# A PEER gather kernel: the dots' second operand in PSUM instead of SBUF, and four PSUM banks for the rest instead of six

## The reference: what is computed

```python
def block(xb):                                   # 128 tokens
    qh = (xb @ wq).reshape(PEER_BLOCK, PEER_HEADS, 2, PEER_HALF)
    s1 = jnp.einsum('thd,nd->thn', qh[:, :, 0], keys1)
    s2 = jnp.einsum('thd,nd->thn', qh[:, :, 1], keys2)
    v1, i1 = lax.top_k(s1, PEER_TOPK)
    v2, i2 = lax.top_k(s2, PEER_TOPK)
    ...                                          # top 16 of the 16 x 16 sums: sc, e
    gate = jax.nn.softmax(sc, axis=-1)
    act = jax.nn.gelu(jnp.einsum('td,thkd->thk', xb, u_tab[e])) * gate
    return jnp.einsum('thk,thkd->td', act, v_tab[e])
```

## Time and profile before

| what | value |
|---|---|
| median of three runs | 3465.75 us (3464.83 to 3470.75) |
| span of the profiled execution | 3605.3 us |
| one block of the loop in it | 404 to 413 us |
| busy share PE, DVE, POOL, ACT | 84%, 65%, 64%, 18% |
| moved by DMA | 1213.76 MB, 337 GB/s over the span |

### The profile page before, as it was taken

The page is one execution under the profiler, slowest core; times in us unless marked ns, Lnnn a source line. Parts: engine busy times, 40 slices in busy tenths (PEclk is TensorE's granted clock), DMA queues, the critical chain, the costliest instruction groups (busy, mean ns, idle before and its releaser), DMA issues.

```text
span 3605.3 us, 39214 instructions
## 1 busy us (share of the span) xinstructions
PE 3011.3 (84%) x10724; PEld 1568.6 (44%) x10724; DVE 2354.0 (65%) x5813; ACT 658.5 (18%) x2015; POOL 2298.7 (64%) x2132
## 2 busy tenths in 40 slices
PE   7687888889987898879987798879987799877677
PEld 2553454345533454345533454345533454344222
DVE  3565975578656875578756876568655876568442
ACT  2211221112211221112211221112211121111111
POOL 0224666766777566766676567667676567667775
PEclk9799999989999999999999999999998999999999
DMA  6456989999999999999999999999999999999998
GB/s 241 161 174 240 366 316 346 371 354 351 337 372 378 348 338 351 348 361 359 330 368 357 363 314 355 361 340 369 341 353 355 364 327 345 350 375 373 355 368 296
DMA packets 340167, 1213.76 MB, mean 337 GB/s; under 512 B 41072, under 2 KB 41200, under 8 KB 339904
## 3 DMA queue, kind: packets, MB, share of 16 engines
q0 software_dynamic: 304128, 1107.43, 83.1%
q1 hardware_dynamic: 35776, 103.32, 7.7%
HBM read 1205.73 MB, written 4.87 MB: 336 GB/s over the span
## 4 chain that ended last, share of the span: by engine, by line
PE 37%; issue 20%; DMA 16%; DVE 9%; POOL 9%; another core or an unknown queue 6%; ACT 3%; POOLq 0%; ACTq 0%; SPq 0%; DVEq 0%
PE acc L428 23%; PE bank L428 13%; DMA ring<-peer_v,idx 11%; POOL ring L404 9%; DMA ring<-peer_u,idx 6%; DVE ring L1266 2%; ACT xn L750 1%; ACT diag L750 1%; DVE kw L1050 1%; DVE xn L1161 0%; DVE xn L1164 0%; ACT h L750 0%; ACT xT L750 0%; DVE topi L1052 0%
## 5 line engine op out<-in xcount | busy, mean ns | idle before, releaser
L428 PE MATMUL acc<-ring,diag 128*128 128x512 f32 (+1 forms) x4224 | 2086.7, 623 | 449.9 <-DMA ring<-peer_v,idx 269.1
L1266 DVE SCALAR_TENSOR_TENSOR ring<-ring,xcur 128x1024 f32<-128x1024 f32 x1056 | 1289.0, 1225 | 818.0 <-DMA ring<-peer_u,idx 744.5
L404 POOL DMA_INDIRECT ring<-peer_v,idx x1056 | 1151.2, 1090 | 643.6 <-issue 291.9
L404 POOL DMA_INDIRECT ring<-peer_u,idx x1056 | 1143.7, 1083 | 642.7 <-issue 316.5
L428 PEld LDWEIGHTS acc<-ring,diag 128*128 128x128 f32 (+1 forms) x4224 | 746.4, 192 | 1427.7 <-issue 1107.3
L750 ACT ACTIVATE diag<-ident,coef 128x128 f32<-128x128 f32 x1024 | 366.7, 395 | 646.7 <-PE acc L428 392.6
L428 PEld LDWEIGHTS bank<-xT,win 128*128 128x128 f32 (+1 forms) x2304 | 272.9, 183 | 79.2 <-issue 73.5
L428 PE MATMUL bank<-xT,win 128*128 128x128 f32 (+1 forms) x2304 | 282.6, 277 | 2.4 <-ACT xT L750 2.4
L750 ACT ACTIVATE G<-bank 128x128 f32<-128x128 f32 (+1 forms) x137 | 40.6, 296 | 830.4 <-PE bank L428 449.4
L428 PE MATMUL bank<-win,xT 128*128 128x512 f32 (+3 forms) x368 | 166.2, 583 | 1.9 <-ACT xT L750 1.9
L428 PEld LDWEIGHTS bank<-xT,qk 128*128 128x128 f32 x1024 | 131.5, 201 | 37.1 <-issue 37.1
(11 more groups left out here) (227 smaller groups left out, 1821.1 us busy)
## 6 DMA issues: line engine op xcount, KB each, us to landing
qk<-wq SPq DMA_DIRECT2D x64, 512.0 KB
t<-wq SPq DMA_DIRECT2D x64, 512.0 KB
ring<-peer_u,idx POOLq DMA_INDIRECT x1056
ring<-peer_v,idx POOLq DMA_INDIRECT x1056
win<-w_in SPq DMA_DIRECT2D x6, 2048.0 KB, 15.1
ring<-wq SPq DMA_DIRECT2D x16, 512.0 KB, 5.1
wout<-w_out SPq DMA_DIRECT2D x1, 4096.0 KB, 22.8
xn<-x_prompt SPq DMA_DIRECT2D x8, 512.0 KB
```

Source lines behind the costliest of these rows:

```text
L404: pool.indirect_dma_start(out=ring[:, slot, :], out_offset=None, in_=(peer_u, peer_v)[which], in_offset=bass.IndirectOffsetOnAxis(ap=idx[: ...
L428: return nc.tensor.matmul(out, lhsT, rhs, start=start, stop=stop)
L1266: stt(row, row, 1.0, xcur[:, :], ALU.mult, ALU.mult, accum_out=dots[:, column(b, e):column(b, e) + 1]).then_inc(s_dot, 1)
```

## The change

`xcur` moves from SBUF to PSUM, where it takes two banks, so that `acc` and `xcur` hold four and `bank` shrinks from six to four. The dot reads one operand from SBUF and one from PSUM; its line is otherwise unchanged. The mixer's tiles are laid anew on four banks (`xl`, the r gate and the polynomial in `bA`, gates, i gate and `v` in `bB`, `gl`, `k`, its transposes and the scores of the mLSTM in `bC`, `q`, the columns and `o` in `bD`), with a wait wherever a bank's last reader now is another one. ACT's exponential of `o` moves from tick `T_CHUNK + 8` to `T_CHUNK + 6`. The query projections use banks 2 and 3, and both halves of a head's scores lie in one bank, so that DVE waits for both in step 0.

```diff
-        xcur = sb("xcur", [P, D_MODEL])
...
+        xcur = ctx.enter_context(nc.psum_tensor("xcur", [P, D_MODEL], fp32))
-        bank = [ctx.enter_context(nc.psum_tensor(f"bank{b}", [P, 512], fp32)) for b in range(6)]
-        bA, bB, bC, bD, bE, bF = bank
+        bank = [ctx.enter_context(nc.psum_tensor(f"bank{b}", [P, 512], fp32)) for b in range(4)]
+        bA, bB, bC, bD = bank
...
                 if tick - T_K in PARTS:
...
+                        if full:
+                            pe.wait_ge(s_gl, w + 1)
-                    last = project_part(v, n, bF, 1536, f, "k")
+                    last = project_part(v, n, bC, 1536, f, "k")
...
                 if full and tick - T_V in WIDE_PARTS:
...
+                        pe.wait_ge(s_ri_exp, v + 1)
...
                 if tick == T_V + 1:
-                        pe.wait_ge(s_gl, w + 1)
+                        pe.wait_ge(s_q, w + 1)
...
                 if full and tick - T_O in WIDE_PARTS:
-                        pe.wait_ge(s_q, w + 1)
+                        pe.wait_ge(s_cols, v + 1)
...
                 if full and tick == T_CHUNK:
-                    pe.wait_ge(s_ri_exp, v + 1)
+                    pe.wait_ge(s_m2, v + 1)
...
                 if full and tick == T_CHUNK + 3:
-                    pe.wait_ge(s_lru, v + 1)
+                    pe.wait_ge(s_kw, v + 1)
...
                 if tick == T_CHUNK + 8:
...
+                    if full:
+                        pe.wait_ge(s_o, w + 1)
...
                 if tick == T_OUT - 2:
                     pe.wait_ge(s_ym, w + 1)
+                    pe.wait_ge(s_c, v + 1)
...
                 if tick == T_NORM2 + 3:
-                    pe.wait_ge(s_c, v + 1)
...
-                        last = mm(bank[4 + half][:, 0:P], wq_buf[half][:, c, :], xT[:, c, :], start=c == 0, stop=c == CM - 1)
+                        last = mm(bank[2 + half][:, 0:P], wq_buf[half][:, c, :], xT[:, c, :], start=c == 0, stop=c == CM - 1)
...
-                    mm(bank[2 * (head % 2) + half][:, 0:P], q2[:, half, :], keysT[:, half, :]).then_inc(s_score, 1)
+                    mm(bank[head % 2][:, P * half:P * half + P], q2[:, half, :], keysT[:, half, :]).then_inc(s_score, 1)
...
-                if full and tick == T_CHUNK + 8:
+                if full and tick == T_CHUNK + 6:
                     act.wait_ge(s_o_ps, w + 1)
-                    act.wait_ge(s_num_ps, w + 1)
-                    a(sigo[0:n, :, :], by4(bE)[0:n, :, :], ACT.Exp, scale=-1.0).then_inc(s_o, 1)
+                    act.wait_ge(s_s_ps, w + 1)
+                    act.wait_ge(s_qd, w + 1)
+                    a(sigo[0:n, :, :], by4(bD)[0:n, :, :], ACT.Exp, scale=-1.0).then_inc(s_o, 1)
...
-                if step < 2:
-                    dve.wait_ge(s_score, b * 16 + 2 * head + 1 + step)
+                if step == 0:
+                    dve.wait_ge(s_score, b * 16 + 2 * head + 2)
                     held()
...
-                pair_of = [bank[2 * (head % 2) + half][:, 0:P] for half in range(2)]
+                pair_of = [bank[head % 2][:, P * half:P * half + P] for half in range(2)]
```

More of the change, by code:

```diff
@@ L468, in mixer @@
                         for c in range(CM):
-                            last = nc.tensor.transpose(by4(bank[4 + c // 4])[:, c % 4, 0:m], xn[0:m, c * P:(c + 1) * P], ident[0:m, 0:m])
+                            last = nc.tensor.transpose(by4(bank[2 + c // 4])[:, c % 4, 0:m], xn[0:m, c * P:(c + 1) * P], ident[0:m, 0:m])
                         last.then_inc(s_xt_ps, 1)
@@ L477, in mixer @@
                             pe.wait_ge(s_topk, 2 + (w - 1) * PEER_HEADS)
-                    last = project_part(v, n, bC, 0, f, "xl")
+                    last = project_part(v, n, bA, 0, f, "xl")
                     if f == FT - 1:
@@ L500, in mixer @@
                         pe.wait_ge(s_win[1], 16)
-                    last = project_part(v, n, bD, 512, f, "gl")
+                    last = project_part(v, n, bC, 512, f, "gl")
                     if f == FT - 1:
@@ L507, in mixer @@
                         pe.wait_ge(s_win[2], 16)
-                    last = project_part(v, n, bE, 1024, f, "q")
+                    last = project_part(v, n, bD, 1024, f, "q")
                     if f == FT - 1:
@@ L532, in mixer @@
                         pe.wait_ge(s_win[4], 16)
+                        pe.wait_ge(s_ri_exp, v + 1)
                     m = BOTH if is_count(v, 0) else n
                     for c in (2 * part, 2 * part + 1):
-                        last = mm(bA[0:m, :], xT[:, c, 0:m], win[:, c, 2048:2560], start=c == 0, stop=c == CM - 1)
+                        last = mm(bB[0:m, :], xT[:, c, 0:m], win[:, c, 2048:2560], start=c == 0, stop=c == CM - 1)
                     if part == 3:
@@ L559, in mixer @@
                         pe.wait_ge(s_win[5], 16)
-                        pe.wait_ge(s_q, w + 1)
+                        pe.wait_ge(s_cols, v + 1)
                     for c in (2 * part, 2 * part + 1):
-                        last = mm(bE[0:n, :], xT[:, c, 0:n], win[:, c, 2560:3072], start=c == 0, stop=c == CM - 1)
+                        last = mm(bD[0:n, :], xT[:, c, 0:n], win[:, c, 2560:3072], start=c == 0, stop=c == CM - 1)
                     if part == 3:
@@ L787, in mixer @@
                     for c in range(CM):
-                        last = a(xT[:, c, 0:m], by4(bank[4 + c // 4])[:, c % 4, 0:m], ACT.Copy, scale=vec[:, nmix][:, c:c + 1])
+                        last = a(xT[:, c, 0:m], by4(bank[2 + c // 4])[:, c % 4, 0:m], ACT.Copy, scale=vec[:, nmix][:, c:c + 1])
                     last.then_inc(s_xt, 1)
@@ L809, in mixer @@
                     act.wait_ge(s_gl_ps, w + 1)
-                    a(G[:, :, 0:n], by4(bD)[:, :, 0:n], ACT.Copy)
-                    a(t3[:, :, 0:n], by4(bD)[:, :, 0:n], ACT.Square).then_inc(s_gl, 1)
+                    a(G[:, :, 0:n], by4(bC)[:, :, 0:n], ACT.Copy)
+                    a(t3[:, :, 0:n], by4(bC)[:, :, 0:n], ACT.Square).then_inc(s_gl, 1)
                 if full and tick == T_GELU + 2:
@@ L830, in mixer @@
                     for f in range(FT):
-                        a(t1[:, f, 0:n], by4(bC)[:, f, 0:n], ACT.Exp, scale=-1.0, bias=neg[:, f:f + 1])
+                        a(t1[:, f, 0:n], by4(bA)[:, f, 0:n], ACT.Exp, scale=-1.0, bias=neg[:, f:f + 1])
                     for f in range(FT):
@@ L841, in mixer @@
                     act.wait_ge(s_v_ps, projected(v))
-                    a(vt[0:m, :, 0:HEAD], by4(bA)[0:m, :, :], ACT.Copy).then_inc(s_v, 1)
+                    a(vt[0:m, :, 0:HEAD], by4(bB)[0:m, :, :], ACT.Copy).then_inc(s_v, 1)
                 if tick == T_LRU + 10:
@@ L868, in mixer @@
                     for f in range(HEADS):
-                        last = a(xc[:, f, 0:n], by4(bF)[:, f, 0:n], ACT.Copy, scale=vec[:, mnorm][:, f:f + 1])
+                        last = a(xc[:, f, 0:n], by4(bC)[:, f, 0:n], ACT.Copy, scale=vec[:, mnorm][:, f:f + 1])
                     last.then_inc(s_ymT, 1)
@@ L893, in query @@
                         act.wait_ge(s_score, b * 16 + ft - 1)
-                    a(q2[:, half, :], bank[4 + half][:, 0:P], ACT.Copy).then_inc(s_q2, 1)
+                    a(q2[:, half, :], bank[2 + half][:, 0:P], ACT.Copy).then_inc(s_q2, 1)
                 if step == 7:
```

30 lines of the change are left out of this document (15 added, 15 removed).

## The result

The changed kernel takes 3381.84 us in the median of four runs (3380.66 to 3388.64), against 3465.29 us of four runs of the kernel before: a ratio of 0.977, with a 95% interval of 0.9742 to 0.9797. That is 83.5 us or 2.4% less. I had predicted 3432 us, 34 us less.

The account below looks back on a forecast made before the run. No engine was full: PE, POOL and DVE, nearly equally loaded, shared a ring and took turns as the bound. Terms -45 + 0 + 10 + 0 = -35 us of 3605.3, -34 us unprofiled, gave 3432 us; eight-in-ten range 3350 to 3480.

Parts of the forecast that it names:

- step 1: DVE's dots, reading xcur from PSUM, stop holding POOL's gathers: 292 us less POOL work, 45 us less time.
- Step 2: The dot's own time on DVE with one PSUM input: -21 to +13 us of DVE's time, taken as 0.
- Step 3: DVE waits for both halves' scores before a head's choice: 10 us more, with 0 and 64 as bounds.
- Steps 4 and 5: The mixer's new waits on four banks: 0, perhaps 8 us against; ACT writing xcur to PSUM nine times: 0.
- half the excess: Rival: half of the gathers' 292 us excess is on the path, giving 3335 us; chance 0.18.
- the gathers were freed: Denies the rival that gathers stay at 1.09 us and only the score wait's 10 us remain: 3475 us, chance 0.06.
- something did follow: Denies the rival that gathers shrink but POOL just waits longer for slots: 3466 us, chance 0.11.
- the score wait decided nothing: Denies the rival that DVE's wait for scores costs 64 us against 15 us of gain: 3513 us, chance 0.12.

Follow-up runs that it names:

- second profile: The kernel before, unchanged, profiled once more: 3459.72 us, ratio 0.9981.
- the kernel with the U row alone: The kernel before with the dot made a one-input instruction that scales and sums the U row, activations left out: 3378.52 us, ratio 0.9769.

## Why the prediction was wrong, step by step

**The mechanism of step 1 was right.** The gathers were to fall to 0.94 or 0.95 us in the mean and are at 0.953; POOL's busy time was to be about 2007 us and is 2015.6; POOL's waits for PE and DVE were to grow by some 200 us and grew by 188. Of the some 25 us of held time that are left in the changed kernel, all but a trace lie with 107 gathers over 1.0 us, and all but one of these start inside another DVE instruction: 5 us lie with `kw<-kw,topi`, 4 with `xn<-h,stat,ffn_bc`, and 19 of the gathers start inside a `TENSOR_SCALAR` with one input.

**The size of step 1 was the error.** I took 45 of 292 us for the path, a share of 0.15. The term measured 80 to 83 us of 262 to 283 (against either profile of before), about 0.3. The step that failed is the working of its bound, the sum of held time on the chain: "A path's end can fall by no more than what of the removed time lies on the chain", which gave 55 us. The same working on the second profile gives 6% of 3453.6 = 207 us of POOL's pieces, and a gather's excess there is 1.077 - 0.941 = 0.136, or 12.6% of it: 26 us. The DMA pieces are 22%, 760 us, some 101 pieces of 7.5 us with 0.136 us each: 14 us. That is 40 us, and the measured gain is twice as much. So the atypical first profile isn't the reason.

The traces show what was miscounted. In the second profile of before, the chain stands on POOL without a break from 1599.96 to 1614.84 us: ten gathers run there one behind the other, 0.30 us apart, and take 11.6 of the 14.9 us. The view of the chain for that stretch gives POOL a quarter of it, and the rest of the gathers stands under `issue`:

```profile
by line: issue 72.6%; POOL ring L404 26.8%; POOLq L402 0.6%
```

In all that execution the page's 6% stand for 210 us of POOL. But the stretches in which the chain is on POOL, its gathers and the `issue` between them, last 558 us; 382 gathers run in them and take 413 us. These gathers are also held more than the average one, by 0.178 us instead of 0.136, 68 us together. The 107 DMA pieces on the chain begin with gathers that are held by 15 us more. The sum is 83 us, not 40. Counted so, the profile that the prediction read has 80 + 16 = 95 us where I had 43 + 12 = 55, and three other kernels whose gathers are held as before, those with the new layout, the broadcast and the score wait alone, have 69 to 77. The measured 80 to 83 us lie among these.

So a bound from the chain was not wrong in kind. I took POOL's share as the page prints it and left the 20% of `issue` at nothing; I gave the chain's gathers the average hold; and I went down from 55 to 45 because gathers on the chain would mostly start with no dot running, while in fact they are held more than the others. Such a sum is an upper bound, and no run shows why the gain should come up to it. What is shown beside it is the price by deliberate change, 0.30 to 0.34 us for each us of POOL's time around this operating point.

**I used one average for stages that differ.** I compared POOL's 33 us of excess in a block of the loop with PE's 350 of 409 us and stayed low, and gave the last block no term. In it PE is busy 266 of 348 us, and PE's sums wait for V rows. This is its group in that window before, and after:

```profile
L428 PE MATMUL acc<-ring,diag 128*128 128x512 f32 x512 | 249.1, 614 | 75.0 <-DMA ring<-peer_v,idx 71.7 <-ACT diag L750 3.2
```

```profile
L428 PE MATMUL acc<-ring,diag 128*128 128x512 f32 x512 | 250.2, 616 | 58.1 <-DMA ring<-peer_v,idx 52.8 <-ACT diag L755 5.2
```

PE's wait for V rows falls by 19 us, and the window by 18. The last block alone gives 17 of some 80 us. For a block of the loop I had put 4 us, and said that much more would make step 1 wrong; the seven blocks show 6.7 in the mean, a fifth of the 34 us freed.

**Step 2, the dot's own time, was right.** 1218 ns against 1224 and 1225 before, inside the bounds of -21 to +13 us (7.4 us less by the groups), and the kernel with the U row alone has 1217. The 125 ns on PSUM against 60 on SBUF that the Trainium skill gives (Perfetto Trace Analysis, Optimizing Scalar/DVE Operations) does not show as a longer dot in this trace.

**Step 3, the score wait, was put at 10 us and measured nothing that shows.** Alone it gave 1.0004, -4 to +7 us, and beside free gathers the change has the ratio of the kernel without it (0.977 and 0.9769). I expected `tops` to wait 50 to 90 us for `bank`; it waits 26.5 us, 18 times, against 8.9 in the second profile of before. The 44 cases and 89 us were read off one trace with its times held fixed; once the wait stood there, 18 cases of it were left. Why the others went stays open.

**Steps 4 and 5 were right.** The new layout with the activations in SBUF gave 0.9988, no cost that can be told from none.

**The rivals.** Of the forms, "half the excess" had the right idea, a shorter gather that pulls all along, with too high a share: 0.3, not 0.5. The time, 3382, lies between its 3335 and my 3432. The other three fell: the gathers were freed, something did follow, and the score wait decided nothing. The forecast said what would break it, that the chain's share of POOL says little of what a shorter gather is worth. That is what happened, but the reason given there, several paths of nearly the same length, isn't shown; what the traces show is that the share was read too small.

**What stays open** is how the 0.3 comes about from the waits of single gathers. The runs show the price, and that it is higher in the last block; the chain counted gather by gather comes near the gain as a whole, but not block by block. In the windows above it has 14 us for the block of the loop, which gained 9, and 12 for the last block, which gained 18.

## What to carry to other kernels

When gathers issued by POOL run beside elementwise work, look at the longest DVE instructions that take two inputs from SBUF: one input moved to PSUM frees POOL, and the gather's median against its mean in the profile says how much there is. Look at one-input instructions as well where they run at 0.43 us for 512 float32 columns from SBUF to SBUF, for those held gathers too. Do not take an engine's share of the chain as the page prints it for all of its work there: look into the chain's stretches, count its instructions with the `issue` pieces between them, and take what each of these would lose, not the average. Then add a little known time to each step of that engine and read the price, which needs no such count. Price the stages apart: here the one without a second load on PE gave about 0.6 for each us freed (0.3 to 0.8 by its time's interval), the loop about a quarter.

## What the runs showed of the hardware that I had not expected

- A `TENSOR_SCALAR` of 512 float32 columns from SBUF to SBUF (0.43 us, one input) holds a gather, 1.10 us instead of 0.94 with 0.29 us of it to go; one of the same size from SBUF to PSUM (0.69 us) doesn't.
- A second input that is one column broadcast over 1024 holds a gather as a full one does: 1.65 us instead of 0.94, and no change in time (0.9997).
- A fill of 0.22 us between two gathers costs only 0.08 us, since most of it runs in the 0.30 us that POOL's sequencer needs for the next gather.
- A microsecond of POOL's time costs 0.30 to 0.34 us between 2656 and 3045 us of work in some 3400. Past that it was 0.56 in one kernel, where holds and clock differ too.
